# Two experts with fixed numbers go first in the expert units of a decoder layer, and all shared down products run beside units

## What is computed

```python
s = jax.nn.sigmoid(x @ w_router); sb = s + router_bias
...                                   # best 4 of 8 groups, then the best 8 experts in them
_, eidx = lax.top_k(jnp.where(emask, sb, -jnp.inf), TOP_K)      # TOP_K = 8
gates = ...                           # scores of the chosen eight, scaled to sum to 2.5
def expert(acc, xs):                  # for each of the 64 experts
    wg, wu, wd, ge = xs               # (1024, 256), (1024, 256), (256, 1024)
    y = (jax.nn.silu(x @ wg) * (x @ wu)) @ wd
    return acc + ge[:, None] * y
shared = (jax.nn.silu(x @ ws_gate) * (x @ ws_up)) @ ws_down
x = layernorm(DEEPNORM_ALPHA * x + gt2 * (routed + shared), ln2_g, ln2_b)
```

```
experts 0 to 63: 20 26 33 12 45 90 72 28 53 35 77 67 91 62 136 95 101 84 36 122 12 36 24 58 11 130 47 24 57 68 41 18
                 58 80 19 85 89 33 110 95 50 41 39 135 24 124 42 129 11 43 98 140 134 137 75 109 30 92 107 58 118 40 44 152
sorted, ranks 0 to 63: 152 140 137 136 135 134 130 129 | 124 122 118 110 109 107 101 98 95 95 92 91 |
                 90 89 85 84 80 77 75 72 68 67 62 58 | 58 58 57 53 50 47 45 44 | 43 42 41 41 40 39 | 36 36 35 33 33 30 |
                 28 26 24 24 24 20 19 18 12 12 11 11
```

## Time and profile before

| | |
|---|---|
| median of 3 runs | 1503.09 us (1498.76 to 1503.31) |
| time of the profiled execution | 1499.84 us |
| its span | 1498.1 us |
| PE busy | 1373.6 us (92% of the span) |
| DVE, ACT, POOL busy | 565.4, 291.3, 313.3 us |
| moved by DMA | 358.52 MB, mean 239 GB/s |

### The profile page before, as it was taken

The page is one execution under the profiler, slowest core; times in us unless marked ns, Lnnn a source line. Parts: engine busy times, 40 slices in busy tenths (PEclk is TensorE's granted clock), DMA queues, the critical chain, the costliest instruction groups (busy, mean ns, idle before and its releaser), DMA issues. The chain is left out here.

```text
span 1498.1 us, 21979 instructions
## 1 busy us (share of the span) xinstructions
PE 1373.6 (92%) x8512; PEld 790.1 (53%) x8512; DVE 565.4 (38%) x1292; ACT 291.3 (19%) x674; POOL 313.3 (21%) x334
## 2 busy tenths in 40 slices
PE   5999999999979999889999799999899999999966
PEld 3775777764657776767454333434343444434322
DVE  2101455453632674435887343211111111212138
ACT  1002333354223222111121001111111111111021
POOL 6000000000059995100045111111111111111000
PEclk9999999999989999989999899999999999999988
DMA  9510410123464442684203999999999999999685
GB/s 338 177 56 26 125 58 1 57 86 113 135 186 140 133 149 87 192 312 149 81 29 96 393 384 421 420 419 405 410 394 406 408 407 412 393 403 392 235 316 228
DMA packets 106805, 358.52 MB, mean 239 GB/s; under 512 B 28837, under 2 KB 31013, under 8 KB 80581
## 3 DMA queue, kind: packets, MB, share of 16 engines
q1 hardware_dynamic: 81288, 301.98, 52.5%
q0 software_dynamic: 15968, 40.61, 7.4%
q10 hardware_dynamic: 9446, 14.51, 2.8%
HBM read 331.49 MB, written 38.15 MB: 247 GB/s over the span
## 5 line engine op out<-in xcount | busy, mean ns | idle before, releaser
L2152 PE MATMUL bank<-arena 128*32 128x512 f32 (+2 forms) x1536 | 331.4, 610 | 20.6 <-DMA arena<-in_w_up 20.3
L2152 PEld LDWEIGHTS bank<-arena 128*32 128x32 f32 (+2 forms) x1536 | 119.3, 137 | 202.0 <-issue 201.2
L2160 PE MATMUL bank<-arena 128*32 128x512 f32 (+2 forms) x768 | 168.1, 597 | 0.9 <-DVE arena L2930 0.9
L2139 POOL DMA_INDIRECT expert_rows<-arena x46 | 46.4, 1008 | 483.4 <-PE bank L2145 384.1
L2924 DVE TENSOR_TENSOR arena<-arena,bank 128x256 f32<-128x256 f32 x46 | 19.4, 421 | 318.6 <-ACT arena L2572 318.6
L1226 PE MATMUL bank<-arena 128*128 128x272 f32 x512 | 131.3, 410 | 8.0 <-DMA arena<-in_w_in 7.4
L454 PE MATMUL bank<-arena 128*128 128x272 f32 x480 | 112.9, 398 | 4.5 <-DVE arena L2014 2.1
L1226 PEld LDWEIGHTS bank<-arena 128*128 128x128 f32 x512 | 97.6, 196 | 34.6 <-issue 12.8
L2160 PEld LDWEIGHTS bank<-arena 128*32 128x32 f32 (+2 forms) x768 | 56.5, 134 | 106.0 <-issue 104.8
L454 PEld LDWEIGHTS bank<-arena 128*128 128x128 f32 x480 | 92.3, 193 | 24.6 <-issue 2.8
L684 PE MATMUL bank<-arena 128*128 128x272 f32 x384 | 99.7, 403 | 0.0
(11 more groups left out here) (485 smaller groups left out, 1787.1 us busy)
## 6 DMA issues: line engine op xcount, KB each, us to landing
arena<-in_w_gate SPq DMA_DIRECT2D x64, 1024.0 KB, 12.9
arena<-in_w_up SPq DMA_DIRECT2D x64, 1024.0 KB, 17.6
arena<-in_w_down SPq DMA_DIRECT2D x64, 1024.0 KB, 16.2
arena<-in_w_ada SPq DMA_DIRECT2D x12, 2048.0 KB, 9.0
arena<-in_w_in SPq DMA_DIRECT2D x11, 2048.0 KB, 10.3
arena<-expert_rows SPq DMA_DIRECT2D x8, 2048.0 KB, 25.4
gate_logits<-arena ACTq DMA_DIRECT2D x16, 272.0 KB, 3.5
arena<-gate_logits SPq DMA_DIRECT2D x8, 544.0 KB, 5.0
```

Source lines behind the costliest of these rows:

```text
L2139: return nc.gpsimd.indirect_dma_start(out=y_d, out_offset=bass.IndirectOffsetOnAxis(ap=rows, axis=0), in_=of, in_offset=None, bounds_check ...
L2152: mm = nc.tensor.matmul(out[rows].rearrange("p (a n) -> p a n", a=2), x[:, k, rows], gate_up_slot(n)[:, :, k, :], start=k == 0, stop=k == ...
L2160: mm = nc.tensor.matmul(out[rows, :], h[:, k, rows], down_slot(n)[:, k, 512 * half:512 * half + 512], start=k == 0, stop=k == 1)
```

## The change

- Experts 0 and 1 (`FIXED`) become units 0 and 1, each alone in a unit of 128 rows. They are sorted behind all others (rank 62 and 63, room 128); the other 62 experts take ranks 0 to 61. `SMALL` becomes 50 and there are five units "N" (`NPAIR`): 2 + 8 + 8 + 12 + 12 + 5 = 47 units, still 64 loads.
- Their weights are loaded behind `ws_down`, before the order is stored. Their row numbers are made on the chip: `first_one_hots` on DVE for each tile, ten products on PE (`first_rows`), `first_indices` on DVE. POOL makes three iotas behind the eight entries of tile 0, and gathers units 0 and 1 before it fetches the lists.
- `unit_rows` and `unit_indices` move behind the gate and up products of unit 0.
- All five shared down products run beside units 2, 3, 4, 5 and 8. Until unit 10 the results use two buffers instead of four.

```diff
-HEAVY, THREE, WIDE, PAIRED, SMALL = 8, 20, 32, 40, 52
+HEAVY, THREE, WIDE, PAIRED, SMALL = 8, 20, 32, 40, 50
+FIXED, NPAIR = (0, 1), 5
+NF, LISTED = len(FIXED), PAIRED + NPAIR
...
+for i in range(NF):
+    LOADS.append(None)
+    UNITS.append((LISTED + i, segments(P, (i, P))))
+for kind in spread(dict(X=8, W=12, T=12, N=NPAIR), 3, 0):
...
-            for rows, cap in ((E, 32.0), (SMALL, 64.0), (WIDE, 96.0), (THREE, 128.0), (HEAVY, 192.0)):
+            step(pool.iota(sort_id, pattern=[[1, 1]], base=0, channel_multiplier=1, **fl))
+            step(pool.iota(sort_id[0:NF], pattern=[[1, 1]], base=int(LAST), channel_multiplier=1, **fl))
+            for rows, cap in ((E, float(P)), (E - NF, 32.0), (SMALL, 64.0), (WIDE, 96.0), (THREE, 128.0), (HEAVY, 192.0)):
...
-    UP_BANK = [6, 0, 1, 6, 0]
+    UP_BANK = [6, 0, 1, 6, 5]
...
-    BESIDE = (2, 3, 4)
+    BESIDE = {2: 0, 3: 1, 4: 2, 5: 3, 8: 4}
...
             load_shared(ws[1], "ws_down")
+            for n, e in enumerate(FIXED):
+                load_expert(sp, n, e, gl[n], dl[n])
             sp.wait_ge(order_done.sem, 1)
...
+            def first_rows():
+                pe.wait_ge(first_made.sem, NT)
+                for i in range(NF):
+                    for t in range(NT):
+                        mm = nc.tensor.matmul(bank[4][:, 256 + i:257 + i], first_hot[t][i][0:TOKS[t]], first_val[i][0:TOKS[t], t:t + 1],
+                                              start=t == 0, stop=t == PT)
+                first_mm.inc(mm)
...
             overflow_sums()
+            first_rows()
             up(3)
             table()
             up(4)
-            unit_rows()
-            down(0)
-            down(1)
...
-            pe.wait_ge(s_hid.sem, NT)
+            pe.wait_ge(s_hid.sem, 3)
             xT(0)
-            pe.wait_ge(s_fold.sem, 1)
+            pe.wait_ge(h2T_sb.sem, 2 * NT)
             for u in range(NU):
                 if u:
                     hiddenT(u - 1)
+                if u - 1 in BESIDE:
+                    shared_step("high", BESIDE[u - 1])
+                gate_up_of(u)
+                if u == 0:
+                    unit_rows()
+                    pe.wait_ge(s_hid.sem, NT)
+                if u == 1:
+                    down_of(0)
                 if u + 1 < NU:
                     xT(u + 1)
...
+            pool.wait_ge(h2_store.sem, 16 * NT)
+            pool.wait_ge(first_done.sem, 1)
+            for u in range(NF):
+                gather_rows(row_buffer(u), from_rows[:, LISTED + u:LISTED + u + 1]).then_inc(first_ld[u].sem, 16)
...
+            def first_one_hots(t):
+                n = TOKS[t]
+                if t == 0:
+                    dve.wait_ge(places_made.sem, 1 + NF)
+                step(TT(place_in[0:n, t, :], key[0:n, t, 0:NF], ebase[0:n, 0:NF], ALU.subtract))
+                step(TT(first_val[1][0:n, t:t + 1], first_val[1][0:n, t:t + 1], selm[0:n, t, 0:1], ALU.subtract))
+                for i in range(NF):
+                    ins = TS(first_hot[t][i][0:n], places[0:n], place_in[0:n, t, i:i + 1], None, ALU.is_equal)
+                    done(first_made, ins) if i == NF - 1 else step(ins)
+
+            def first_indices():
+                dve.wait_ge(first_mm.sem, 1)
+                cols = slice(LISTED, NU)
+                step(TS(units_f[:, cols], bank[4][:, 256:256 + NF], float(FILL), None, ALU.add))
+                done(first_done, row_indices(step, *(v[:, cols] for v in (units_f, floor_f, to_rows, from_rows))))
...
             layernorm(4)
+            first_one_hots(0)
+            first_one_hots(1)
+            first_one_hots(2)
             choose(3)
...
             order_and_excess()
+            first_one_hots(3)
+            first_one_hots(4)
             shared_hidden(0)
             shared_hidden(1)
+            first_indices()
             residual(3)
             residual(4)
```

More of the change, by code:

```diff
@@ L75, in spread @@
     return order
-heavy, wide, three, pairs = iter(range(HEAVY)), iter(range(HEAVY, THREE)), iter(range(THREE, WIDE)), iter(range(PAIRED, PAIRED + 6))
-for kind in spread(dict(X=8, W=12, T=12, N=6), 3, 0):
+heavy, wide, three, pairs = iter(range(HEAVY)), iter(range(HEAVY, THREE)), iter(range(THREE, WIDE)), iter(range(PAIRED, LISTED))
+for i in range(NF):
+    LOADS.append(None)
+    UNITS.append((LISTED + i, segments(P, (i, P))))
+for kind in spread(dict(X=8, W=12, T=12, N=NPAIR), 3, 0):
     n = len(LOADS)
@@ L2092, in build @@
     ov_to, ov_from = at(T2 + 4 * NU + 2, 1, dt=U32), at(T2 + 4 * NU + 3, 1, dt=U32)
-    BESIDE = (2, 3, 4)
+    BESIDE = {2: 0, 3: 1, 4: 2, 5: 3, 8: 4}
     sd_low, s_low = Tick(nc, "shared_down_low"), Tick(nc, "shared_folded_low")
     NPE = 6
+    Y_OF = [u % 2 if u < max(BESIDE) + 3 else u % RY for u in range(NU)]
+    y_turn = lambda u: 16 * Y_OF[:u].count(Y_OF[u])
     halves = lambda off: (at(off, 4, D), at(off + 4 * D, 4, D))
@@ L2101, in build @@
     TAIL = [PT, 0, 1, 2, 3]
+    first_hot = [[at(T1 + 1024 + P * (NF * t + i), P) if t < PT else at(T2 + 1024 + P * i, P) for i in range(NF)] for t in range(NT)]
+    places, place_in = at(T2 + 1280, P), at(T2 + 1408, NT, NF)
+    first_val = [at(T2 + 1408 + NF * NT + NT * i, NT) for i in range(NF)]
+    assert T2 + 1408 + 2 * NF * NT <= WS0 and NF * PT * P <= 1024
+    row_buffer = lambda u: Yb[u] if u < NF else Xg[(u - NF) % RX]
     rows_s = at(T2 + 2 * D, 2, D)
@@ L2116, in build @@
     dup_done, unit_mm, unit_done = (Tick(nc, n) for n in ("lists_doubled", "unit_rows_in_psum", "unit_rows_done"))
+    places_made, first_made, first_mm, first_done = (Tick(nc, n) for n in ("places_made", "first_one_hots", "first_rows_in_psum", "first_rows_done"))
+    first_ld = [Tick(nc, f"first_tokens_gathered{i}") for i in range(NF)]
     g_ld = [Tick(nc, f"tokens_gathered{i}") for i in range(RX)]
@@ L2283, in up @@
                     su_mm.inc(mm)
[L2285 to L2305, removed]
             def counts():
@@ L2397, in xT @@
                         pe.wait_ge(free.sem, u)
[L2398 removed]
+                    transpose_rows(half, row_buffer(u)).then_inc(xt_mm.sem, 1)
             def gate_up_of(u):
@@ L2654, in scatter @@
                 col = UNITS[u][0]
[L2655 to L2657 removed]
+                scatter_rows(to_rows[:, col:col + 1], Yb[Y_OF[u]]).then_inc(y_out[Y_OF[u]].sem, 16)
             pool.wait_ge(unit_done.sem, 1)
             pool.wait_ge(su_mm.sem, PT)
[L2660 removed]
+            for u in range(NF, NF + RX):
                 gather(u)
[L2662 to L2666 removed]
+            for u in range(1, NU):
+                if u + NF + RX - 1 < NU:
+                    gather(u + NF + RX - 1)
+                scatter(u - 1)
             scatter(NU - 1)
             for j in range(RY):
[L2669 removed]
+                pool.wait_ge(y_out[j].sem, 16 * Y_OF.count(j))
             def late(i):
```

155 lines of the change are left out of this document (72 added, 83 removed).

## The result

| | before | with the change |
|---|---|---|
| median | 1502.38 us (4 runs, 1498.76 to 1503.31) | 1562.44 us (4 runs, 1561.31 to 1565.07) |
| profiled execution, span | 1498.1 us | 1563.4 us |
| ratio | | 1.041, 95% interval 1.039 to 1.043 |

What follows compares the result with a forecast made beforehand. PE (busy 92%) bounds the kernel, DMA close behind, loads pacing PE a little. From 1499.84 us: entry -12.6, PE work +22.2, waits -15.3 (together -5.7), overflow +45.3, giving 1539 us, range 1520 to 1575.

Steps and rivals of the forecast that it cites:

- three signs of being wrong: Profile after: no late instruction, units ending later than before, or POOL's stretch behind the late scatter much over 9 us.
- The signs of the late unit itself: Profile after: late instructions behind the last unit, 65 issues per weight matrix instead of 64, 3.1 MB more DMA.
- The late unit itself: Behind the last ordinary unit: one overflow unit for one token, in series from SP's loads to scatter and landing, 36.5 us.
- The empty rounds: Late loop behind the late unit: POOL's 35 other rounds at 0.25 us each, 8.8 us, bounds 3.5 and 28.
- my 45.3: Behind the last ordinary unit: late unit 36.5 us plus 35 rounds 8.8 us, uncovered; low 37, high 77.
- The rival of dear rounds: Late loop: jumps fetch code, so rounds cost 24 to 70 us, total 1555 to 1600, about 1575; chance 0.12.
- The entry: Routing to unit 0: rows no longer wait for lists; unit 0 starts at 830.5, 12.6 us earlier.
- The one about `table`: End of routing: `overflow_rows` is late, so `table` on PE waits for it about 1 us.
- PE's work: Ordinary units: one more unit, two more shared products, `unit_rows`, `unit_indices`, less unit 0's slow start: +22.2 us.
- The waits for weights: PE's waits for gate and up weights in the units: 5 of 20.3 us left, so -15.3 us.
- The rival that the entry gives nothing: Unit 0 held back to 843 or loads pacing units as before: 13 to 15 us more, 1553; chance 0.13.
- No late unit: Overflow behind the units: no row over its room, the 45.3 us fall away, 1494 us, faster; chance 0.05.

Runs made afterwards that it cites:

- experiment 1: Changed kernel with rooms moved by one rank, so rank 50 has 64 rows and no late unit runs: 1511.5 us; repeated 1509.4 us, ratio 1.007.
- experiment 2: Kernel before, room of rank 50 counted as 32 rows: one late unit, 1563.0 us, ratio 1.031; from rank 49: two late units, 1602.0 us.
- second profile of the change: Profile of the changed kernel run once more, unaltered, beside its variant with rooms that fit: 1561.7 us, ratio 1.041.
- Experiment 4: Variant of experiment 1 with the next unit's row transposes again ahead of the shared product's second half from unit 2 on: 1501.7 us, ratio 1.001.
- experiment 6: Order stored from ACT's queue, on Experiment 5's variant: 1502.9 us, repeated 1501.2 us, ratio 1.000; stored between early loads, on Experiment 4's: 1507.3 us, ratio 1.000.
- Experiment 5: Variant of Experiment 4 with both fixed experts in one unit, 46 units: 1500.6 us, ratio 0.999; repeated 1499.3 us, ratio 0.999.

## Why the prediction was right or wrong

**The direction and the cause were right, several sizes were not.** The forecast was 1539 us in a range of 1520 to 1575; 1562.4 lies in the range and 23 us above the forecast. It lies outside 1524 to 1552, which the forecast had for itself. The wide range holds it only because it was drawn to take in two rivals, and neither of them happened as described, so that it lies in the range is in part luck. The slowdown is 60 us where I had 36. The late unit was read from the counts of the reference and the table of rooms: rank 50 with 33 rows in a room of 32. Experiments 1 and 2 show it from both sides, 52.3 us taken away and 50.2 us put in.

Of my three signs of being wrong two came up. POOL's stretch behind the late scatter is 17.7 us, not 9. And the ordinary units end later than before, not 6 us earlier: the last ordinary scatter is at 1440.7 instead of 1425.1, of which 6.8 us arose ahead of the change. Unit 0's products start at 840.12 instead of 830, and the waits for `in_w_up` are over 10 us. The signs of the late unit itself, 65 loads and 3.16 MB more, came as named.

**The late unit itself: right.** I had 36.5 us; the second late unit of experiment 2 follows the first after 36.4, and in the change 36.8 lie between the last ordinary scatter and the late one. The steps agree too: gate and up products 8.98 us for 8.9, the transposes 1.97 for 1.94, and from SP's issue to the list rows 10.0 for 10.5. The clock was the reason for the first two: behind 19.2 us without work PE's granted clock was 0.56 on average from 1458 to 1466, at the lower level at first (weight loads of 0.34 us) and at the upper from 1465.4 on (0.19 us).

**The empty rounds: mis-sized.** "I take 0.25 us a round, 8.8 us" was 0.43 us and 15.2 us. I added the durations of branches; but in a round of POOL the recorded instructions take 0.16 us in sum (0.05, 0.03, 0.03 and 0.045), and the rest lies between them, where no duration shows it. PE's rounds take (1498.4 - 1472.4) / 35 = 0.74 us. They end 3 us behind SP's first load for the final sum, whose data PE needs only at 1502.8. By the figures of the Trainium skill (Advanced Engine Details and Errata, Control Flow Timing), two compare-and-branches of 108 ns and a branch of 51 ns a round, it would have been 9.3 us, an estimate; the measured rounds are dearer, and the measurement decides. The whole late part is still only 3.8 us over my 45.3, which is in part luck: 36.8 and 15.2 make 52.0, and 49.1 was measured. Behind the late scatter of one row POOL's rounds begin after 2.2 us, while before, behind a full scatter, POOL's load of the count began after 4.1 and SP's loads after 5.4; so 2.5 us stand in the place of 5.4, which I had not subtracted. The rival of dear rounds named a mechanism, a fetch of code at every jump, that gave 24 us or more; the rounds of all five engines came to 0.43 to 0.74 us, so of the rule of the Trainium skill (Runtime: NRT & Kernel Launch, Instruction fetch mechanics) that a taken branch out of the loaded pages stalls, this loop shows no clear sign.

**The entry: -9.8 us for -12.6.** The steps that I named are there: waits of PE for DVE of 2.29, 0.63 and 0.75 us (3.3 in sum without the 0.35 that was there before; I had 2.5), and `first_rows` with 2.65 us for 1.7. The one about `table` was wrong: PE had lost so much ahead of it that it hardly waited. What I didn't have is that the products of tile 3 behind `first_rows` took 8.83 us, where the same sixteen of the same shape took 7.13 before. The -9.8 rests on one profile of each kernel; against the entries of experiment 2 (56.4 and 55.7) it would be about -16.

**PE's work: some 24 to 27 us for 22.2.** The units' stretch is 18.6 us longer with 8.0 us less of waits for weights; in the second profile of the change it is 15.2 longer with 9.2 less. The step that failed is "two halves of 1.98 and a gap of 0.46": I priced a shared product beside a unit by the old loop, in which the row transposes of the next unit cover DVE's reading of bank 7. The change moves them behind the gate and up products, and the gap is 1.28 us, five times, 4.1 us more than 0.46. The 2 us for `unit_indices` were right: 2.33. Unit 0 gave its slow start back (7.11 us for 8.94), but unit 1's products now took 8.53 us where 7.1 is usual. The order printed ahead of the prediction showed this move only for the first units, and I didn't ask what the moved transposes had hidden. Experiment 4 puts them back and wins 7.7 us, more than this wait explains.

**The waits for weights: 12.3 us left, not 5.** "I take 5 us of the 20.3 as left" was too hopeful by 7.3 us. The two experts loaded ahead helped the following loads little: the first load by rank went out later than before (830.14, that is 30.3 us behind the last store of token rows, against 16.2), because the store of the order stood behind the early weights. The load after that left 39.4 us behind the last store, against 39.3 for the same one before. That shortening this wait wins nothing clear of the spread was shown in experiment 6; what holds most loads is the slots, which PE frees (SP waits 377 us for PE's last products on a slot, 383 before). Experiment 5 shows the same balance from the other side.

**The rivals.** The rival that the entry gives nothing has the size but not the mechanism: instead of -5.7 us for everything but the late unit, +7.8 came out (experiment 1), a miss of 13.5 us where the rival had 13 to 15. But unit 0 did come earlier, and the waits for weights did fall. My bounds for that sum, about -13 and +7, don't follow from its terms: with 0 and 20.3 us of waits left they are -10.7 and +9.6. No late unit: excluded, and the dear rounds, 1555 to 1600 by fetched code, too: a round of POOL at 0.43 us is below their 0.68. Of the 23 us between forecast and median, the units' part takes 11.7, the late part 3.8, the entry 2.8; the rest is the scale, as the sum started from an execution of 1499.8 us where the median is 1502.4, and what the two profiles' first halves differ by.

## What to carry to other kernels

When a kernel gives ranks fixed rooms before it knows the data, a change of the table must be read against the sorted counts: here one row over one room cost 50 us, some six times as much as everything else in the change, and a table shifted by one rank avoids it. Where a fallback stands in a loop of fixed length, price the empty rounds by the spacing of its instructions, not by their durations, and bound the loop by what can occur. And where work is moved, ask what it covered: the row transposes moved behind the gate and up products uncovered five waits.

## What the runs showed of the hardware that was not expected

- **A busy PE at a lower clock.** Behind the ten products of one column (`first_rows`, 2.65 us) PE did not idle, yet in the profile of the change the granted clock was 0.81 on average in the next 9 us, and weight loads that took 0.19 us before and behind took 0.33 us in four places. Busy time by stretch of the change (the seventh number group is the clock):

```profile
820.00:826.00 6.00, 6.00 (x32) 4.06 (x31) 1.90 (x8) 0.39 (x1) 3.83 (x4) 1.00 0.99 215
826.00:835.00 9.00, 9.00 (x24) 3.70 (x24) 7.55 (x20) 0.39 (x1) 3.22 (x3) 0.81 0.70 162
```

  The cause is open. The products behind took 8.83 us in five of the seven profiles with these ten products, and 7.13 in the other two (both of the variant whose rooms fit, experiment 1). They took 7.13 in all four profiles in which the ten have weights of 64 columns and take 1.58 us, and in all three of the kernel before and its variants. So the fall was seen only behind the ten products with 128 columns, but they don't always bring it.
- **A small store behind large loads.** The 256 bytes of `expert_by_rank` made SP wait 11.2 us behind the early weights on the same queue (7 MB, the first of which had landed by then). The Trainium skill (DMA: Bandwidth & Descriptors, Queues, rings and completion order) says that each DMA engine takes the descriptors of a ring in order; the trace agrees, with 0.8 us when no load was left ahead of it. That is not all: on ACT's queue, with none of these loads ahead of it, SP read the order 7.2 and 8.3 us behind the store's issue (experiment 6).
